# Decays of the scan and of the forget-gate attention as fp32r products of 32 rows of running sums

## The reference, cut to what matters

```
cum = jnp.cumsum(log_f, axis=1).transpose(0, 2, 1)
logits = jnp.einsum("bqhd,bkhd->bhqk", qb, kb) * scale
logits = logits + cum[:, :, q0:kl, None] - cum[:, :, None, :kl]
p = jax.nn.softmax(jnp.where(k_pos[None, :] <= q_pos[:, None], logits, NEG_INF), axis=-1)
outs.append(jnp.einsum("bhqk,bkhd->bqhd", p, vb))
```

```
decay_in = jnp.exp(segsum(a))      # out[i, j] = sum of a[j+1..i] for i >= j, else exp(-inf) = 0
cb = jnp.einsum('bclgn,bcsgn->bgcls', Cc, Bc)
y_diag = jnp.einsum('bgcls,bgrcls,bcsgrp->bclgrp', cb, decay_in, x_dt)
```

## Time and profile before

| what | value |
|---|---|
| median of three runs | 1449.78 us |
| the profiled execution's own time | 1451.42 us |
| its span, first to last instruction | 1449.7 us |
| granted TensorE clock, mean of the span | 0.996 |
| PE busy | 1419.8 us (98%) |
| DVE busy | 1082.9 us (75%) |
| ACT busy | 793.9 us (55%) |
| POOL busy | 71.5 us (5%) |
| chain that ended last, shares | PE 87%, DVE 8%, ACT 3% |

### The profile page before, as it was taken

One profiled execution on the slowest core, in us unless ns is written; L12 is line 12 of the kernel. 1 busy time (PEld: TensorE's weight loads), 2 busy tenths in 40 slices (PEclk: granted clock), 3 DMA queues, 4 the chain that ended last, 5 costly groups with the idle time before them and its releaser, 6 DMA issues.

```text
span 1449.7 us, 25954 instructions
## 1 busy us (share of the span) xinstructions
PE 1419.8 (98%) x8633; PEld 1255.3 (87%) x8633; DVE 1082.9 (75%) x2053; ACT 793.9 (55%) x1307; POOL 71.5 (5%) x68
## 2 busy tenths in 40 slices
PE   8999999999999999999999999999999999999998
PEld 8977878888898887799999999888888888788886
DVE  6997776666688588599999997566666666667776
ACT  6755764545576435455555445455555555545444
POOL 0000000000001562000000000000000000000000
PEclk9999999999999999999999999999999999999999
DMA  7523335655345423554656887657557575667753
GB/s 291 193 102 117 130 126 185 196 188 188 131 146 178 144 85 115 182 182 146 204 186 223 253 257 258 217 186 248 190 187 252 186 256 188 198 223 248 252 196 145
DMA packets 103354, 274.57 MB, mean 189 GB/s; under 512 B 8176, under 2 KB 41072, under 8 KB 102784
## 3 DMA queue, kind: packets, MB, share of 16 engines
q1 hardware_dynamic: 64832, 237.11, 49.2%
q10 hardware_dynamic: 38176, 34.63, 7.3%
q0 software_dynamic: 288, 2.10, 0.5%
HBM read 254.93 MB, written 18.87 MB: 189 GB/s over the span
## 4 chain that ended last, share of the span: by engine, by line
PE 87%; DVE 8%; ACT 3%; issue 1%; POOL 1%; DVEq 0%; ACTq 0%; POOLq 0%
PE Y L1954 44%; PE AO L1954 39%; PE M L1954 2%; DVE wl L1054 2%; ACT wh L490 1%; DVE I L1603 1%; DVE SCO L1619 1%; DVE I L1617 1%; ACT xhl L533 0%; PE M L2044 0%; DVE X L1270 0%; DVE V L1625 0%; DVE V L1611 0%; DVE xn L1267 0%; PE M L2318 0%
## 5 line engine op out<-in xcount | busy, mean ns | idle before, releaser
L1054 DVE TENSOR_TENSOR wl<-raw,wh 128x1024 fp32r<-128x1024 f32 x440 | 545.2, 1243 | 199.8 <-ACT wh L490 199.3
L1954 PE MATMUL AO<-xhl,wh 128*128 128x256 f32 (+3 forms) x2784 | 649.7, 316 | 5.3 <-DVE wl L1054 2.5
L490 ACT CAST wh<-raw 128x1024 fp32r<-128x1024 f32 x440 | 461.0, 1050 | 142.4 <-PE Y L1954 75.7
L1954 PEld LDWEIGHTS AO<-xhl,wh 128*128 128x128 f32 x2784 | 456.2, 189 | 38.0 <-issue 2.8
L1954 PE MATMUL AO<-xhl,wl 128*128 128x256 f32 (+2 forms) x1776 | 485.2, 282 | 0.0
L1954 PEld LDWEIGHTS AO<-xhl,wl 128*128 128x128 f32 x1776 | 334.4, 188 | 7.9
L1954 PE MATMUL Y<-wh,peer_ah 128*128 128x512 f32 x512 | 199.9, 390 | 3.1 <-DVE peer_al L1751 3.1
L1954 PE MATMUL Y<-wh,peer_al 128*128 128x512 f32 x512 | 200.0, 391 | 0.0
L1954 PE MATMUL Y<-wl,peer_ah 128*128 128x512 f32 x512 | 199.9, 390 | 0.0
L972 ACT CAST peer_ah<-hid 128x256 fp32r (+1 forms) x128 | 52.0, 406 | 182.7 <-DVE hid L1745 95.9
L1954 PEld LDWEIGHTS Y<-wh,peer_ah 128*128 128x128 f32 x512 | 96.6, 189 | 21.5 <-DVE peer_al L1751 2.3
(11 more groups left out here) (330 smaller groups left out, 1623.8 us busy)
## 6 DMA issues: line engine op xcount, KB each, us to landing
raw<-in_stream SPq DMA_DIRECT2D x440, 512.0 KB, 3.3
gate_spill<-gstage ACTq DMA_DIRECT2D x32, 512.0 KB, 5.0
gates<-gate_spill ACTq DMA_DIRECT2D x6, 2048.0 KB, 15.1
gates<-gate_spill ACTq DMA_DIRECT2D x8, 512.0 KB, 6.9
rowg<-in_post SPq DMA_DIRECT2D x3, 512.0 KB, 4.3
X<-in_x SPq DMA_DIRECT2D x2, 512.0 KB, 4.8
memx<-in_mem SPq DMA_DIRECT2D x1, 1024.0 KB, 7.6
keys<-in_keys POOLq DMA_DIRECT2D x1, 1024.0 KB, 7.1
```

The costliest lines, as they stand in the source:

```text
L490: nc.scalar.copy(wh[:, s, :], raw[:, s, :]).then_inc(split_hi, 1)
L1054: nc.vector.tensor_tensor(wl[:, s, :], raw[:, s, :], wh[:, s, :].bitcast(F32), ALU.subtract)\
L1954: return nc.tensor.matmul(o, a, b, start=start, stop=stop)
```

## The change

It replaces the way in which the decays are formed, and moves one product of the attention from DVE to ACT. All of it stands below, cut to its core.

1. Attention. PE forms running sums of `log_f` for both roundings (high and rest) in one 32-row tile at j = 5 of "qk": three float32 products with 32 output rows. ACT copies it rounded (`FH`), DVE forms the operand `FS` from it; two DMAs of POOL's queue put the sums of 8 heads side by side on two rows of `FV`. `FV`'s other rows hold a selection (+1 where the row is the head's), written by one ACT copy of 32x2048 ahead of `first_tap(3)`. Then one fp32r product of 32 rows replaces the float32 products with `DEC`, whose 24 activations go.
2. `ident` and the masks become fp32r (the fill 2^100), so that their product is one matmul.
3. `probabilities` of the six forget-gate groups: DVE keeps the reciprocal, ACT does the product with it, ahead of its split.
4. Scan. Two 128-column float32 products at the end of PE's small products form the running sums, ACT copies them rounded (`RH`), DVE forms `RS`, 16 DMAs on SP's queue fill rows of `RV`, an ACT copy of 128x768 after the mlp writes `RV`'s selection. `seg(k)` becomes an fp32r product of 32 rows plus one of `ident` with the mask `RM`. POOL's 16 products `AU` go.
5. Semaphores are merged (`meta_ss` into `norm_ss`, `mv_out` into `v_out`, `numbered` and `ranked` into `indexed`).

```
 ACT, before the phase "qk":
+            act.wait_ge(picked, 3)
+            nc.scalar.activation(FV[0:ROWS_OF, :, :], row_pick[0:ROWS_OF, LO_ROW + FOX_H:LO_ROW + 2 * FOX_H][:, :, None]
+                                 .to_broadcast([ROWS_OF, FOX_H, T]), ACT.Copy).then_inc(picked, 1)
             first_tap(3)
 ACT, in "qk" and "v":
-                    forget_decays(0, 4 * (j - 6), 4 * (j - 5))
+                if j == 5:
+                    act.wait_ge(f_prod, 2)
+                    nc.scalar.copy(FH[0:ROWS_OF, :], Y[0:ROWS_OF, 1, 512:512 + T]).then_inc(line_hi, 1)
-                forget_decays(1 + j // 2, 4 * (j % 2), 4 * (j % 2) + 4)
 ACT, attention loop, ahead of its split:
+            def probabilities(g):
+                act.wait_ge(at_inv, g + 1)
+                for i, (_, _, n) in enumerate(members(g)):
+                    p = att_p[:, g % 2, n * i:n * i + n]
+                    ins = nc.scalar.activation(p, p, ACT.Copy, scale=peaks(g, 32, i))
+                ins.then_inc(at_p, 1)
 ACT, after the mlp, and after the exponents in "xbc":
+            nc.scalar.activation(RV[:, :, :], row_pick[:, LO_ROW + FOX_H:LO_ROW + FOX_H + HG][:, :, None]
+                                 .to_broadcast([P, HG, P]), ACT.Copy).then_inc(picked, 1)
             meta_high()
+            nc.scalar.copy(RH[:, :, :], M[:, 1, P:3 * P].rearrange("p (c l) -> p c l", c=2)).then_inc(line_hi, 1)
 DVE, at its start: three reductions and sums of ident into row_pick; in forget(1):
-                    nc.vector.tensor_tensor(zf, z8, zf, ALU.subtract).then_inc(logf, 1)
+                    for r in (0, LO_ROW):
+                        nc.vector.tensor_tensor(FA[:, :, r:r + FOX_H], zf, z8, ALU.subtract).then_inc(line_cols, 1)
 DVE, at j == 6 of "qk": FS, 32x256, from FH and Y; in the attention loop:
-                    probabilities(s)
+                    inverse_sums(s)
 DVE, after dt_a:
+            dve.wait_ge(dt_a, 2)
+            dve.wait_ge(line_cols, 7)
+            for r in (0, LO_ROW):
+                nc.vector.tensor_copy(
+                    RA[:, :, :].rearrange("p c (g r) -> p c g r", r=ROWS_OF)[:, :, :, r:r + HG],
+                    dtz[:, 3, 24:72].rearrange("p (c g r) -> p c g r", c=2, g=SSD_G)).then_inc(line_cols, 1)
 DVE, after the second xdd_w: RS, 128x256, from RH and M
 SP, at the third block of "z": lines(), 16 DMAs of one row of RV each, from 6 rows of RS
 PE, at j == 5 of "qk":
+                    mm(o[:, 0:P], FA[:, 0, :], upper[:, :], True, True)
+                    mm(o[:, P:], FA[:, 0, :], ones[:, :], True, False)
+                    mm(o[:, P:], FA[:, 1, :], upper[:, :], False, True).then_inc(f_prod, 1)
 PE, logits(g):
-                    if kind == "first":
-                        mm(o, upper[:, :], d[:, :, 0, :], True, False)
-                    else:
-                        mm(o, upper[:, :], d[:, :, 1:3, :].rearrange("p a n k -> p a (n k)"), True, False)
-                        mm(o[:, :, 0:P], ones[:, :], d[:, :, 0, :], False, False)
-                    mm(o[:, :, w - P:], ident[:, :], mask[:, None, :].to_broadcast([P, n, P]), False, False)
+                    mm(o, FS[0:ROWS_OF, q], FV[0:ROWS_OF, first:first + 2 * n - 1:2, 0:w], True, False)
+                    mm(o[:, :, w - P:], ident_r[:, :], mask[:, None, :].to_broadcast([P, n, P]), False, False)
 PE, small products of "xbc":
+            pe.wait_ge(line_cols, 9)
+            for c in range(2):
+                ins = mm(M[:, 1, P * (c + 1):P * (c + 2)], RA[:, c, :], upper[:, :], True, True)
 PE, seg(k):
-                mm(AO[:, 0, 0:3 * P], later[:, :], AU[:, k % 2, :, :].rearrange("p a b -> p (a b)"),
-                   True, True).then_inc(seg_prod, 1)
+                mm(AO[:, 0, 0:3 * P], RS[r, c, :], RV[r, h, :].rearrange("p a b -> p (a b)"), True, False)
+                mm(AO[:, 0, 0:3 * P].rearrange("p (a b) -> p a b", a=3), ident_r[:, :],
+                   RM[:, None, :].to_broadcast([P, 3, P]), False, True).then_inc(seg_prod, 1)
 POOL: memsets and selects of FA, RA and RM; two DMAs into FV; decay_inputs(k) goes, skip_and_gate(0, 0..2) follow each other
```

More of the change, by code:

```diff
@@ L184, in build @@
         rowg = at("rowg", [P, 3, D], 8768)
-        mask = at("mask", [P, P], 21056)
+        mask = at("mask", [P, P], 21056, F32R)
         memx = at("memx", [P, TT, D], 22080)
@@ L465, in _, with lines @@
             fetch((STREAM["mq"] // SLOTS, STREAM["z"] // SLOTS), 0, lambda i, s: i * SLOTS + s)
+            def lines():
+                sp.wait_ge(picked, 5)
+                sp.wait_ge(line_lo, 2)
+                for g in range(SSD_G):
+                    for c in range(2):
+                        for n, r in ((0, 0), (1, LO_ROW)):
+                            o, f = ROWS_OF * g + ONE_ROW + 2 * c + n, ROWS_OF * g + r
+                            sp.dma_start(RV[o:o + 1, :, :].bitcast(F32), RS[f:f + HG, c, :].bitcast(F32)).then_inc(lines_in, 16)
             for n in range(24):
                 b = STREAM["z"] + n
+                if n == 2:
+                    lines()
                 sp.wait_ge(split_lo, b - 3)
@@ L1715, in _ @@
             dve.wait_ge(top_T, TT)
-            dve.wait_ge(numbered, 1)
             def one_hots(c):
@@ L1857, in _ @@
                 inverse_root(stat[:, 8 + k:9 + k], stat[:, k:k + 1], D, norm_rstd)
+            pool.wait_ge(picked, 4)
+            pool.wait_ge(line_lo, 1)
+            for n, r in ((0, 0), (1, LO_ROW)):
+                o = FOX_ONE_ROW + n
+                pool.dma_start(FV[o:o + 1, :, :].bitcast(F32), FS[r:r + FOX_H, :].bitcast(F32)).then_inc(fox_in, 16)
             pool.wait_ge(consts, 8)
@@ L1925, in skip_and_gate @@
                     .then_inc(pool_gate, 1)
-            for k in range(2, 16):
-                decay_inputs(k)
-                if k in SKIP_AT:
-                    skip_and_gate(*SKIP_AT[k])
+            for p in range(3):
+                skip_and_gate(0, p)
             group_norm(0)
@@ L2303, in _ @@
             mm(M[:, 1, 72:96], ones[:, :], a1, True, True)
-            mm(M[0:META, 1, 96:120], later[0:META, 0:META], a0, True, True).then_inc(ac_prod, 1)
+            mm(M[0:META, 1, 96:120], later[0:META, 0:META], a0, True, True)
+            pe.wait_ge(line_cols, 9)
+            for c in range(2):
+                ins = mm(M[:, 1, P * (c + 1):P * (c + 2)], RA[:, c, :], upper[:, :], True, True)
+            ins.then_inc(ac_prod, 1)
             xbc_groups(3, XBC_T // 4)
@@ L2307, in _ @@
             pe.wait_ge(ac_exp, 2)
+            pe.wait_ge(line_lo, 2)
             turned = turned_tiles()
```

144 lines of the change are left out of this document (95 added, 49 removed).

## The result

The changed kernel takes 1455.51 us, median of six executions (1453.1 to 1458.58), against 1450.2 us (1448.0 to 1450.96) for the kernel before, in the same comparison. The ratio is 1.0039, 95% interval 1.0029 to 1.0049: it is slower, by 5.3 us in this comparison where 2.7 were forecast (1452.5), and above the upper end of the range (1455.0). The profiled execution took 1454.01 us, span 1452.3. Most steps of the prediction show in it as foretold. Three things show in it that are in no step.

The account below looks back on a forecast made before the run. The prediction took DVE to set the attention loop's end and PE's own chain the scan's. Its terms 0.9 + 0.55 + 0.6 + 0.7 = +2.7 us on 1449.78 gave 1452.5 us, range 1447.0 to 1455.0.

Parts of the forecast that it names:

- What bounds the kernel: Attention loop ends with DVE's list of work; the scan's chain is PE's own with a few DVE pieces.
- (a): Attention: ACT's copy into `FV` stands where DVE waits for ACT, nothing hides it; +1.8 us (1.6 to 2.2).
- (b): Attention: DVE gets one more small product in `forget(1)`, 0.1, and `FS`, 0.4; +0.5 us.
- (c): Attention loop: the probabilities' product leaves DVE, but DVE then waits for ACT's `mixh`; -1.4 us (-4.3 to 0).
- (d): Attention: the two DMAs into `FV` start some 8 us before `logits(0)`, covered unless they need over 7 us.
- After the mlp and "xbc": `RV` copy delays `meta_high`, +0.55 us (0.3 to 0.8); small DVE copies and `RH` in "xbc", +0.6 (0.2 to 1.0).
- the sentence on SP: In "xbc", the 16 DMAs take their place in SP's order; blocks are fetched several blocks ahead of use.
- Scan: Seg 0.76 us for 0.65, less waits and the late `MM`; sum +0.7 us, bounds -4.7 to +2.4.
- rival A: Scan: changing to 32 rows and back costs an fp32r product nothing, seg 0.36; whole 1447.1 us; chance 0.13.
- B: Attention loop is not held by ACT: (c) is -4.3, the time 1449.6 us; chance 0.11.
- C: ACT becomes the attention loop's bound, between reciprocal and `mixh`; 1453.9 us, or 1454.3 with nothing gained; chance 0.20.
- D: DMAs come late or a part doesn't do what it says: `logits(0)` waits; chance 0.02.

Follow-up runs that it names:

- e4_prob: The changed kernel with the product that makes probabilities of the exponentials back on DVE in all groups; 1457.69 us, ratio 1.0056 to the kernel before.
- e6_moved: The changed kernel with both copies of ones on POOL, the 16 DMAs spread over z's fetches and six stationary tiles moved; 1449.22 us, ratio 0.9991.
- e1_shift: The kernel before with an unused tile of 27 floats ahead of the arena, moving it by 128 bytes; 1450.44 us, ratio 1.0005.
- e11_fv_act: e6_moved with the copy of ones into `FV` put back on ACT, ahead of `first_tap(3)`; 1452.54 us, ratio 1.0018 to the kernel before.
- e7_seg128: The changed kernel with seg's first product over all 128 rows instead of 32, sums wrong, only times of use; 1451.02 us, ratio 1.0006.
- e3_spread: The changed kernel with SP's 16 DMAs into `RV` one behind each of z's fetches 3 to 18; 1455.58 us, ratio 1.0037.
- e2_behind: The changed kernel with `row_pick` behind the arena, so no arena tile moves against the kernel before; 1455.86 us, ratio 1.0039.

## Why the prediction was wrong, step by step

The steps that were costed came out near their figures. What failed is what the sum put at nothing: that all that the diff doesn't compute keeps its pace (1.5 us, shown), that the 16 DMAs on SP's queue cost nothing (0.4 us in the profiled execution, shown), and that a pause of PE costs nothing behind it (some 0.9 us by the clock, an estimate; which pause is at fault is not shown).

**What bounds the kernel.** Right. DVE's list sets the attention's end, and PE's relief gave nothing there up to mv 3 (e4_prob).

**Attention.** (a) The `FV` copy: +1.8 foretold, +1.79 measured, and taken back by e6_moved. (b) +0.5 foretold, +0.48 measured. (c) -1.4 foretold. With these tiles where they were before, v 3 to mq 0 is 75.00 us in e6_moved (20.86, 17.82, 36.33) against 76.16: -1.2. The steps were foretold as 6.47, 6.36, 5.99 and 6.47; they took 6.47, 6.37, 5.98 and 6.72, so the last is 0.25 off. Steps 0 and 1 saved 0.8 and 0.7, and s = 6 0.3 where 0.4 was foretold. (d) Right, nobody waited for POOL's two DMAs.

**After the mlp and "xbc".** +0.55 and +0.6 foretold. xbc 1 to 5 without a fall is 20.27 us (+0.73) and 19.69 with `RV` on POOL, so the copy cost 0.58. xbc 5 to 12 gives +0.3, and 0.3 more lies between xbc 12 and z 9 with the DMAs spread. Together 1.3, where 1.15 was foretold. The step that failed is the sentence on SP: "a block is fetched several blocks ahead of its use". True, but 12 us on the queue are more than that. No row of before had the time that such a DMA takes on the queue, and I gave it none and no bound. It cost 0.4 us here, and 0.7 to 1.0 in three kernels like it. With it "xbc" and "z" came to 1.0 us, the upper bound of that sum.

**Scan.** Seg 0.76 foretold, 0.74 measured, and 0.35 without the mode's change where rival A had 0.36. The late `MM` at 540 is gone, as foretold. Sum foretold +0.7; the two stretches against e1_shift, whose tiles lie the same, give +0.75 and -0.38, so +0.4.

Against e1_shift, whose tiles lie as those of the changed kernel, the loop is -1.3, and these steps make +3.1 us: 1.8 + 0.5 - 1.3, then 0.7 + 0.3 for the copy and "xbc", 0.7 from xbc 12 to z 9 with its 0.4 for the DMAs, and 0.4 for the scan. The sum had +2.7. Up to here the prediction was right, within its own bounds.

**What was not in the sum.** The tiles that the change moves without naming them: +1.5 us by the stretches of e1_shift, +1.6 by its executions at the same clock. The sum 0.9 + 0.55 + 0.6 + 0.7 had no term and no bound for a stage that the change doesn't compute in. The diff shows the cause, a new tile ahead of `arena`, and I read past it: I costed the instructions that change, not the addresses of those that don't. And the granted clock, lower by about 0.001 on average, an estimated 0.9 us (0.6 to 1.3 by the three averages of before). With these it is 3.1 + 1.5 + 0.9 = 5.5 us, and 5.3 to 5.7 was measured; with the last term an estimate, so close a sum is in part luck. The step of the working that failed here is what it says of PE at the `FV` copy: "it is the engine with time to spare in this stage, so I charge nothing for that". That a pause can cost behind it had no term. Which pause it is stays open: the changed kernel's profiled execution has its only fall in these stages behind the copy into `RV`, and e11_fv_act, which tests the `FV` copy, didn't settle it.

**The rivals.** A fell (e7_seg128: the surplus is the mode's). B and C fell with the steps' 6.47 us. D was right in kind, a DMA that comes late, but for "z" and not for `logits(0)`; the signs of being wrong name it, PE waiting for a fetched block in "z", without a price.

## What to carry to other kernels

Read a diff for what it moves, not only for what it computes: a tile of 108 bytes ahead of the arena changed the pace of matmuls that it has nothing to do with, by 2 to 3%. Where time appears in a stage that the change doesn't touch, compare distances between like instructions in both traces, stage by stage; they mostly repeat to within a tenth of a microsecond, while whole executions differ by 2 to 5. And look at what stands beside a product before giving it fewer rows: between products of 128 rows, rows filled with zeros took 0.35 us where 32 rows took 0.74.

## What the runs showed of the hardware

A float32r matmul of 512 columns follows the last at 226.7 ns when its stationary tile lies at remainder 128 to 256 bytes, at 231 to 233 with remainder 0 and at 233.3 with 192. In the other output products the mean distances go the same way: with `mixh` and `mixl` 227 to 229 (128) and 232 to 233 (0), with `m2h` and `m2l` 233 to 234 (192) and 226 to 232 (64).

A DMA of six rows into one, 3 KB, holds SP's queue for 0.75 us (12.05 for 16), longer than the fetch of a block of 512 KB, 0.47 (1.86 for four that leave one behind the other).

TensorE's clock fell to 1.2 GHz behind some of its pauses, at different ones in different executions. A fall cost from nothing (in the attention loop, where DVE sets the end) to 2.5 us (behind the `FV` copy in e3_spread). e2_behind, 1.8 us faster than the changed kernel in the mlp, lost as much again with seven falls.

Going from products of 128 rows to one of 32 and back cost PE 0.39 us, nearly all of it ahead of the 32-row product's start (0.42 us behind the product before it, where one of 128 rows starts after 0.03).
